# Five raw and three upper-half places for the weight blocks, 42 tokens on gathered rows, and spilled activations at a 1536-byte pitch

## The chip, the core and the metric

The kernel runs on one core of one Trainium2 chip. The metric is the device time of the whole program in microseconds. Three timed runs of the kernel before gave a median of 1625.37 us (1622.57 to 1626.13).

The engines are called as in the profile: PE (TensorE, matrix products), DVE (VectorE), ACT (ScalarE), POOL (GpSimd) and SP (SyncE, which here only issues DMAs). Each runs its own instruction stream in order and waits for the others through counting semaphores.

## The reference, cut to what matters

One decoder layer on 512 tokens of 1024 channels in float32: a mixer (a gated short convolution and an HGRN2 recurrence) with one input and one output projection, a cross-attention into 256 memory tokens, a PEER channel mixer, and a final RMSNorm. The change is in how PEER's first product is shared out; for every token `x`:

```python
q = (tokens @ w_query).reshape(Ntok, 8, 2, 128)
s = einsum('nhpd,hpkd->nhpk', q, sub_keys)          # 16 lists of 128 scores for each token
s_top, i_top = lax.top_k(s, 16)                     # best 16 of each list
cand = s_top[:, :, 0, :, None] + s_top[:, :, 1, None, :]
best, pos = lax.top_k(cand.reshape(..., 256), 16)   # 16 experts of each of 8 heads, of 16384
gate = softmax(best)
a = gelu(sum_d x[n, d] * expert_down[idx[n, k], d]) # one "down" dot product for each chosen expert
out[n] = sum_k gate[n, k] * a[n, k] * expert_up[idx[n, k]]
```

Each token thus needs 128 down dot products (8 heads by 16 experts).

## The kernel before, in words

**Two ways to the same dot products.** The last 128 tokens are "sparse": their chosen rows of `expert_down` and `expert_up` are gathered from HBM by indirect DMAs that POOL issues (one row of 4 KB for each of 128 partitions, 512 KB a gather), and DVE multiplies and sums them. The first 384 tokens are "dense": PE multiplies them by *all* 16384 rows, in 128 blocks of 128 experts, and a matrix of gates that is zero for the experts not chosen picks out what counts. A third group, the EDGE = 32 last of the dense tokens, takes the down products from gathered rows and only the up products from the dense path: for them PE's first product is left out, so that its moving side has DE = 384 - 32 = 352 columns in place of 384.

**The precision.** A float32 product is made of three products of halves: upper by upper, upper by lower, lower by upper (function `three`, L1471 to L1475). So each weight block of 128 by 1024 is loaded raw by SP (`load_block`, `load_down`), then ACT writes its upper half (`high`, L580), POOL its lower half, raw minus upper (`low`, L460), and PE uses both in 24 matmuls (8 chunks by 3, `columns`). Raw, upper and lower places form rings of RING = 4 each, all by block number modulo 4. SP may load block p when block p - 4 has been used; ACT may write the upper half of block p when block p - 4 has been used, but its instruction stands behind one that waits for block p - 3.

**The order of the work.** There is no scheduler: the order is written out by hand, an engine at a time.
- The front (mixer, attention, query projection): 92 weight blocks. 84 are split in halves; 8 are used raw.
- PEER's first product: blocks 0 to 127 of `down`, called first-product blocks here. The first 60 (AHEAD) run while DVE chooses the experts of the three dense tiles (`choose`, with dot products of gathered rows put between its steps). PE transposes the chosen indices of a tile when DVE has them (`turn_indices`, L1790): after block 39, and just before block 59. Blocks 60 to 107 alternate with 48 gate steps (`gate_step`, L1762; DVE builds its one-hot operands in `hots`, L1322 to L1327, at most three steps ahead of PE, and ACT stores the gates to HBM). Blocks 108 to 127 stand alone. ACT applies GELU to each block's result and stores the first 112 to HBM (`hid_dram`), 16 stay on chip.
- PEER's second product: 128 blocks of `up`, 18 matmuls of 512 columns each.

**The dot products of gathered rows** (`dots` on DVE, L1184, `down_row` on POOL, L492). There are ROWS = 128 + 128/4 = 160: 128 for the sparse tokens, and 32 for the edge tokens, whose 32 rows stand four times in the 128 partitions, each copy with a quarter of the 128 experts. A table says how many dots follow each step on DVE, and POOL issues its gathers by the same table: 66 during the choosing (ring A of 7 places), 80 in the gate steps (`DOTS_STEP`), and 14 in blocks 108 to 121, one each (`DOTS_END`). In the last two parts ring B has 4 places: POOL issues 4 rows ahead, and gather k waits until dot k - 4 is done. The instructions of one engine that follow a waiting one wait too: POOL's `low` of the next block stands behind the gathers.

**Storage.** `at(kb, ...)` places a tile at a KB offset in a partition. Two tiles, `kept` (44 KB) and `under_w` (16 KB), hold the raw ring and, beneath the names `w_high` and `w_low`, the halves.

## Time and profile before

| | us |
|---|---|
| median of three timed runs | 1625.37 |
| the profiled execution, its own time | 1627.24 |
| its span, first to last instruction | 1625.5 |
| PE busy | 1601.3 (99%) |
| DVE busy | 1141.6 (70%) |
| POOL busy | 827.5 (51%) |
| ACT busy | 670.8 (41%) |

The span leaves 1.7 us of the execution's own time outside. A matmul's record is longer than the distance to the next one's start, since matmuls overlap in the array; so durations of PE are not added up, and the distance from start to start is what one costs. The granted TensorE clock is 1.00 of 2.4 GHz in every stretch. The transfers move 424.69 MB, 261 GB/s over the span, but unevenly: about 110 GB/s in the front and above 300 GB/s from 520 us on.

### The profile page before, as it was taken

What the parts mean: (1) busy time and instruction counts of PE and PEld (TensorE: products, weight loads), DVE (VectorE), ACT (ScalarE), POOL (GpSimd) and SP (SyncE); (2) the same over time, 40 slices, a digit from 0 to 9 for tenths busy, and PEclk for the clock granted to TensorE, in tenths of its full rate; (3) what the DMA queues carried; (4) which work ended last, traced back from release to release, by engine and by line L of the source; (5) the groups of instructions that cost most, each with busy time, mean ns of one, the idle gap of its engine ahead of it and who ended that gap; (6) DMA issues with size and microseconds to landing.
All of it is one profiled execution on the core that took longest, in us unless ns stands there. A gap on an engine that the chain in (4) does not pass through costs nothing.

```text
span 1625.5 us, 26549 instructions
## 1 busy us (share of the span) xinstructions
PE 1601.3 (99%) x9227; PEld 1423.1 (88%) x9227; DVE 1141.6 (70%) x2214; ACT 670.8 (41%) x998; POOL 827.5 (51%) x523
## 2 busy tenths in 40 slices
PE   8999999999999999999999999999999999999998
PEld 6888888888889999999999999998888888888886
DVE  4155451351519998997999898329888888888887
ACT  5342443441434343534544544334333333333333
POOL 4463386413244988987877777766422222222220
PEclk9999999999999999999999999999999999999999
DMA  4222243313434999997999999949999999999992
GB/s 183 95 99 78 76 146 104 104 40 129 143 104 156 344 324 315 327 327 234 336 403 397 394 408 391 359 149 385 400 358 346 336 348 336 346 337 346 339 334 76
DMA packets 154425, 424.69 MB, mean 261 GB/s; under 512 B 15728, under 2 KB 65904, under 8 KB 154224
## 3 DMA queue, kind: packets, MB, share of 16 engines
q1 hardware_dynamic: 89088, 229.41, 40.5%
q0 software_dynamic: 41472, 151.01, 25.5%
q10 hardware_dynamic: 23792, 43.33, 6.9%
q8 instruction: 42, 0.69, 0.2%
q14 instruction: 31, 0.25, 0.1%
HBM read 379.88 MB, written 43.25 MB: 260 GB/s over the span
## 4 chain that ended last, share of the span: by engine, by line
PE 62%; issue 16%; POOL 10%; DVE 7%; DMA 4%; ACT 1%; POOLq 0%; DVEq 0%; SPq 0%; ACTq 0%
PE psum L1473 19%; PE psum L1474 19%; PE psum L1475 19%; POOL w_low L460 8%; PE psum L1762 4%; DMA kept<-down_in 2%; DVE arena L1184 2%; POOL arena L492 1%; DMA gate_dram<-arena 1%; DMA arena<-down_rows,kept 1%; DVE arena L1204 1%; DVE arena L1195 1%; DVE arena L1196 1%; DVE arena L1260 1%; DVE arena L1191 0%
## 5 line engine op out<-in xcount | busy, mean ns | idle before, releaser
L460 POOL TENSOR_TENSOR w_low<-kept,w_high 128x1024 fp32r<-128x1024 f32 x212 | 519.6, 2454 | 319.0 <-ACT w_high L580 317.1
L1473 PE MATMUL psum<-hT_high,w_high 128*128 128x352 f32 (+2 forms) x1408 | 485.7, 345 | 10.8 <-POOL w_low L460 9.4
L1474 PE MATMUL psum<-hT_low,w_high 128*128 128x352 f32 (+2 forms) x1408 | 477.1, 339 | 0.0
L1475 PE MATMUL psum<-hT_high,w_low 128*128 128x352 f32 (+2 forms) x1408 | 476.5, 338 | 0.0
L580 ACT ACTIVATE w_high<-kept 128x1024 fp32r<-128x1024 f32 x212 | 224.1, 1058 | 223.3 <-DMA kept<-down_in 118.5
L1474 PE MATMUL psum<-up_low,wgt_high 128*128 128x512 f32 x768 | 298.8, 389 | 0.0
L1473 PE MATMUL psum<-up_high,wgt_high 128*128 128x512 f32 x768 | 298.8, 389 | 0.0
L1475 PE MATMUL psum<-up_high,wgt_low 128*128 128x512 f32 x768 | 298.8, 389 | 0.0
L1473 PEld LDWEIGHTS psum<-hT_high,w_high 128*128 128x128 f32 x1408 | 264.5, 188 | 30.4 <-POOL w_low L460 15.1
L1475 PEld LDWEIGHTS psum<-hT_high,w_low 128*128 128x128 f32 x1408 | 265.2, 188 | 12.7
L1474 PEld LDWEIGHTS psum<-hT_low,w_high 128*128 128x128 f32 x1408 | 264.9, 188 | 12.3 <-issue 0.5
L584 ACT ACTIVATE up_high<-arena 128x1024 fp32r<-128x1024 f32 x128 | 135.8, 1061 | 311.7 <-PE psum L1475 305.8
L1184 DVE CUSTOM_DVE_ANT_0 arena<-arena,psum 128x1024 f32<-128x1024 f32 x160 | 190.9, 1213 | 48.9 <-DMA arena<-down_rows,kept 48.7
L1355 DVE TENSOR_TENSOR up_low<-arena,up_high 128x1024 fp32r<-128x1024 f32 x128 | 156.8, 1225 | 76.2 <-ACT up_high L584 76.2
L1475 PEld LDWEIGHTS psum<-up_high,wgt_low 128*128 128x128 f32 x768 | 144.2, 188 | 30.0
L1473 PEld LDWEIGHTS psum<-up_high,wgt_high 128*128 128x128 f32 x768 | 144.2, 188 | 29.8
L1474 PEld LDWEIGHTS psum<-up_low,wgt_high 128*128 128x128 f32 x768 | 144.2, 188 | 29.8
L538 POOL DMA_INDIRECT arena<-up_in,kept x64 | 70.0, 1094 | 180.1 <-DVE kept L1363 166.7
L492 POOL DMA_INDIRECT arena<-down_rows,kept x128 | 121.8, 951 | 67.6 <-DVE kept L1184 37.1
L538 POOL DMA_INDIRECT kept<-up_in,kept x64 | 70.9, 1108 | 166.3 <-DVE kept L1363 157.9
L821 ACT ACTIVATE arena<-psum 128x352 f32<-128x352 f32 x112 | 51.6, 461 | 116.3 <-PE psum L1475 109.2
L1327 DVE TENSOR_TENSOR arena<-arena,psum 128x3072 bf16<-128x3072 bf16 x48 | 83.7, 1744 | 0.0
(252 smaller groups left out, 1960.1 us busy)
## 6 DMA issues: line engine op xcount, KB each, us to landing
kept<-down_in SPq DMA_DIRECT2D x128, 512.0 KB, 6.9
arena<-up_in SPq DMA_DIRECT2D x128, 512.0 KB, 5.6
kept<-front_w SPq DMA_DIRECT2D x92, 512.0 KB, 3.4
gate_dram<-arena ACTq DMA_DIRECT2D x40, 512.0 KB, 10.2
hid_dram<-arena ACTq DMA_DIRECT2D x112, 176.0 KB, 7.0
arena<-hid_dram SPq DMA_DIRECT2D x112, 176.0 KB, 5.0
under_w<-gate_dram SPq DMA_DIRECT2D x24, 640.0 KB, 8.4
arena<-gate_dram SPq DMA_DIRECT2D x8, 640.0 KB, 8.3
```

Of the source, the lines that this page charges most:

```text
L460: nc.gpsimd.tensor_tensor(w_low[:, s, :], ring[:, s, :], w_hi[:, s, :].bitcast(F32), ALU.subtract).then_inc(low_ready, 1)
L492: nc.gpsimd.indirect_dma_start(ring[slot], None, down_rows, bass.IndirectOffsetOnAxis((edge_idx if edge else idx3)[:, j:j + 1].bitcast(U32 ...
L538: nc.gpsimd.indirect_dma_start(rows_c[k % RING_C], None, up_rows, bass.IndirectOffsetOnAxis(idx3[:, k:k + 1].bitcast(U32), 0))\
L580: nc.scalar.activation(w_hi[:, s, :], ring[:, s, :], ACT.Copy).then_inc(high_ready, 1)
L584: nc.scalar.activation(up_hi[:, s % 4, :], uraw[:, up_slot(s), :], ACT.Copy).then_inc(up_high, 1)
L1184: nc.vector.tensor_tensor_reduce(ring[slot], ring[slot], h_row, 1.0, 0.0, ALU.mult, ALU.add, (edge_dot if edge else dot3)[:, j:j + 1]).the ...
L1327: nc.vector.tensor_tensor(hot_g[:, s], hot_i.rearrange("p (n q) i r -> p n q i r", q=1).to_broadcast(each), pieces[:, m:m + PAIRS].rearran ...
L1355: nc.vector.tensor_tensor(up_lo[:, up_slot(s), :], uraw[:, up_slot(s), :], up_hi[:, s % 4, :].bitcast(F32), ALU.subtract).then_inc(up_low, 1)
L1473: nc.tensor.matmul(out, lhs[0], rhs[0], start=first, stop=False)
L1474: nc.tensor.matmul(out, lhs[0], rhs[1], start=False, stop=False)
L1475: return nc.tensor.matmul(out, lhs[1], rhs[0], start=False, stop=last)
L1762: ins = nc.tensor.matmul(psum[:, (2 * h + m) % 3, t % 4 * P:(t % 4 + 1) * P], hot_j[:, h % HOTS, t // 2, :, t % 2], hot_g[:, h % HOTS, t / ...
```

## The change

- **Rings.** The raw ring has five places (RING = 5), the upper halves have three (HIGHS = 3), the lower halves five. A block's place comes from its position p in the order of loads, modulo 5 or modulo 3. SP may load block p when block p - 5 has been used; ACT may write the upper half of block p when block p - 3 has been used. The loops of SP, ACT, POOL and PE over blocks are written out.
- **Edge tokens.** EDGE is 42 in place of 32. 128 partitions hold three copies of 42 tokens (PARTS = 3), so each copy has 43 of the experts (the last 42), and there are 43 edge gathers: ROWS = 171. DE is 342. Edge dots and their operands use 126 partitions (84 in the last one).
- **Where the dots stand.** 70 during the choosing (66, and 4 after the third choice: `DOTS_LULL`), 76 in the gate steps, 25 in blocks 108 to 120, two each and one in the last. GELU of the edge dots comes at gate step 16 (was 12), their use at 23 (was 20).
- **Lower halves on DVE.** For blocks 109, 111, 113, 115 and 117 DVE makes the lower half, not POOL (`dve_low`), with a semaphore of its own.
- **Spilled activations.** `hid_dram` has rows of 384 floats (1536 bytes), of which 342 are written and read; before, rows of 352 (1408 bytes).

```diff
-RING = 4
+RING, HIGHS = 5, 3
-EDGE = 32
+UP_FIRST = 4
+EDGE = 42
 PARTS = P // EDGE
-EDGE_SLOTS = SLOTS // PARTS
+EDGE_SLOTS = -(-SLOTS // PARTS)
-GEL_AT, SPLIT_AT, LAST_TURN = 12, 20, 28
+GEL_AT, SPLIT_AT, LAST_TURN = 16, 23, 28
-DOTS_A = DT * (sum(DOTS_SCORES) + sum(DOTS_CAND) + DOTS_HOT)
-DOTS_STEP = (0, 0) + (2,) * 10 + (1, 2, 2) * 12
-DOTS_END = (1,) * 14
+DOTS_LULL = 4
+DOTS_A = DT * (sum(DOTS_SCORES) + sum(DOTS_CAND) + DOTS_HOT) + DOTS_LULL
+DOTS_STEP = (0, 0, 1) + (2, 2, 1) * 15
+DOTS_END = (2, 2) * 6 + (1,)
...
+        def dve_low(i):
+            return DURING <= i < DURING + 10 and i % 2 == 1
...
+            def load_weights(p):
+                weights = front_w[p if p < FRONT else p + RAW0 - FRONT] if p < USED else down_in[p - USED]
+                if p >= RING:
+                    sp.wait_ge(block_used, p + 1 - RING)
+                sp.dma_start(ring[:, p % RING, :], weights).then_inc(wt[p % RING], 16)
...
-            def high(b, s, landed):
-                act.wait_ge(wt[s], landed)
-                nc.scalar.activation(w_hi[:, s, :], ring[:, s, :], ACT.Copy).then_inc(high_ready, 1)
+            def high(p):
+                act.wait_ge(wt[p % RING], 16 * (p // RING + 1))
+                if p >= HIGHS:
+                    act.wait_ge(block_used, p + 1 - HIGHS)
+                nc.scalar.activation(w_half(p)[0], ring[:, p % RING, :], ACT.Copy).then_inc(high_ready, 1)
...
             for i in range(AHEAD + 2, NK):
-                low(FRONT + i, i % 4)
+                if not dve_low(i):
+                    low(FRONT + i)
                 for _ in range(DOTS_STEP[i - AHEAD] if i < DURING else DOTS_END[i - DURING] if ... else ROWS):
...
+            kd = dots(kd, DOTS_LULL)
...
-            kd = dots(kd, ROWS - kd)
+            for i in range(DURING, DURING + len(DOTS_END)):
+                if dve_low(i):
+                    dve.wait_ge(high_ready, FRONT + i + 1)
+                    high, lower = w_half(USED + i)
+                    nc.vector.tensor_tensor(lower, ring[:, (USED + i) % RING, :], high.bitcast(F32), ALU.subtract)\
+                        .then_inc(end_low_ready, 1)
+                kd = dots(kd, DOTS_END[i - DURING])
...
-    args.append(nc.dram_tensor("hid_dram", (NK, P, DE), F32, kind="Internal").ap())
+    args.append(nc.dram_tensor("hid_dram", (NK, P, DN), F32, kind="Internal").ap())
```

POOL, before, from the `low` of first-product block 108 on (L460 is a lower half, L492 a gather of one expert row for each partition):

```order
L460 TENSOR_TENSOR w_low<-kept,w_high 128x1024 [waits high_ready]
L492 DMA arena<-down_rows,kept 128x1024 [waits dot_done]
L460 TENSOR_TENSOR w_low<-kept,w_high 128x1024 [waits high_ready]
L492 DMA arena<-down_rows,kept 128x1024 [waits dot_done]
L460 TENSOR_TENSOR w_low<-kept,w_high 128x1024 [waits high_ready]
L492 DMA arena<-down_rows,kept 128x1024 [waits dot_done]
```

POOL, in the changed kernel, from the same block on (L470 is the lower half, L499 the gather):

```order
L470 TENSOR_TENSOR w_low<-kept,w_high 128x1024 [waits high_ready]
L499 DMA arena<-down_rows,kept 128x1024 [waits dot_done] x4
L470 TENSOR_TENSOR w_low<-kept,w_high 128x1024 [waits high_ready]
L499 DMA arena<-down_rows,kept 128x1024 [waits dot_done] x4
L470 TENSOR_TENSOR w_low<-kept,w_high 128x1024 [waits high_ready]
L499 DMA arena<-down_rows,kept 128x1024 [waits dot_done] x4
```

The lower half of an even block now stands behind four gathers, each with a wait for a dot product; that of an odd block is no longer on POOL.

DVE, before, from the last one-hot operand of the gate steps on (L1327; L1184 is a dot product with its accumulator read, `ISA` here):

```order
L1327 TENSOR_TENSOR arena<-arena,psum 128x3072 [waits dve_step]
L1184 ISA arena,kept<-arena,psum 128x1024 [waits ld_down_rows_b2]
L1184 ISA kept 128x1
L1184 ISA arena,kept<-arena,psum 128x1024 [waits ld_down_rows_b3]
L1184 ISA kept 128x1
L1184 ISA arena,kept<-arena,psum 128x1024 [waits ld_down_rows_b0]
```

DVE, in the changed kernel, from the same place (L1336 is the operand, L1191 the dot product, L1359 the lower half of block 109):

```order
L1336 TENSOR_TENSOR arena<-arena,psum 128x3072 [waits dve_step]
L1191 ISA arena,kept<-arena,psum 128x1024 [waits ld_down_rows_b3]
L1191 ISA kept 128x1
L1191 ISA arena,kept<-arena,psum 128x1024 [waits ld_down_rows_b0]
L1191 ISA kept 128x1
L1191 ISA arena,kept<-arena,psum 128x1024 [waits ld_down_rows_b1]
L1191 ISA kept 128x1
L1359 TENSOR_TENSOR w_low<-kept,w_high 128x1024 [waits high_ready]
L1191 ISA arena,kept<-arena,psum 128x1024 [waits ld_down_rows_b2]
```

A lower half that PE needs now stands behind dots that wait for gathers, and four dots stand between one such half and the next.

## Rows read from the trace of the kernel before

**Rows 1.** The page: busy time of each engine.
```profile
PE 1601.3 (99%) x9227; PEld 1423.1 (88%) x9227; DVE 1141.6 (70%) x2214; ACT 670.8 (41%) x998; POOL 827.5 (51%) x523
```

**Rows 2.** Windows: length, then PE, PEld, DVE, ACT, POOL busy; clock, DMA share, GB/s.
```profile
0.00:520.00 520.00, 509.75 (x2683) 433.55 (x2684) 213.65 (x435) 217.44 (x351) 229.85 (x111) 1.00 0.33 109
520.00:759.00 239.00, 232.29 (x1424) 227.56 (x1424) 223.82 (x779) 100.89 (x133) 205.26 (x124) 1.00 0.92 316
759.00:1018.00 259.00, 258.60 (x2336) 252.26 (x2336) 239.76 (x318) 126.91 (x199) 199.34 (x135) 1.00 1.00 381
1018.00:1097.00 79.00, 78.50 (x490) 77.70 (x488) 22.21 (x40) 30.64 (x45) 55.00 (x30) 1.00 0.70 250
```

**Rows 3.** Timeline of PE: start, duration in us, line, operation, shape.
```profile
481.73 0.33 PE L1473 MATMUL psum<-hT_high,w_high 128*128 128x384 f32 x1
...
501.49 0.33 PE L1473 MATMUL psum<-hT_high,w_high 128*128 128x384 f32 x1
...
534.75 0.43 PE L1473 MATMUL psum<-hT_high,w_high 128*128 128x352 f32 x1 [0.63 <-POOL w_low L460]
...
538.69 0.32 PE L1473 MATMUL psum<-hT_high,w_high 128*128 128x352 f32 x1
...
557.89 0.32 PE L1473 MATMUL psum<-hT_high,w_high 128*128 128x352 f32 x1
...
735.94 0.32 PE L1473 MATMUL psum<-hT_high,w_high 128*128 128x352 f32 x1
...
1299.83 0.39 PE L1475 MATMUL psum<-up_high,wgt_low 128*128 128x512 f32 x1
...
1322.50 0.39 PE L1473 MATMUL psum<-up_high,wgt_high 128*128 128x512 f32 x1
```

**Rows 4.** Waits, 540 to 759 us: waiter and releaser: total us, times, longest.
```profile
ACT w_high L580 <- DMA kept<-down_in: 85.7, 43, 4.5
...
PEld psum L1473 <- POOL w_low L460: 8.2, 14, 1.3
...
DVE arena L1184 <- DMA arena<-down_rows,kept: 4.6, 2, 3.0
```

**Rows 5.** Timeline of POOL, among the first 60 blocks.
```profile
646.50 0.95 POOL L492 DMA_INDIRECT arena<-down_rows,kept  x1 [0.16 <-issue]
647.75 0.93 POOL L492 DMA_INDIRECT arena<-down_rows,kept  x1 [0.30 <-issue]
...
651.27 0.96 POOL L492 DMA_INDIRECT arena<-down_rows,kept  x1 [0.16 <-issue]
```

**Rows 6.** Timeline: DVE's last piece of the third choice, and PE's turn of it.
```profile
750.55 0.29 DVE L1294 TENSOR_TENSOR arena<-psum,arena 128x128 f32<-128x128 f32 x1
...
759.14 0.71 PE L1790 MATMUL psum<-kept,arena 128*128 128x128 f32 x5
```

**Rows 7.** A window of the gate steps, and its gathers: count, us to landing.
```profile
860.00:920.00 60.00, 60.00 (x530) 58.55 (x529) 57.07 (x76) 29.20 (x47) 45.48 (x33) 1.00 1.03 400
...
arena<-down_rows,kept POOLq DMA_INDIRECT x20, 8.8
```

**Rows 8.** DMA issues, 1018 to 1060 us: count, KB each, us to landing; then every gather's.
```profile
kept<-down_in SPq DMA_DIRECT2D x10, 512.0 KB, 4.5
...
arena<-down_rows,kept POOLq DMA_INDIRECT x9, 7.5
...
DMA to landing us min/median/max: 4.3/8.3/11.4
```

**Rows 9.** Timeline at the end of the gate steps: DVE's dots, PE's block 108.
```profile
1007.90 1.21 DVE L1184 CUSTOM_DVE_ANT_0 arena<-arena,psum 128x1024 f32<-128x1024 f32 x1
...
1018.25 0.41 PE L1473 MATMUL psum<-hT_high,w_high 128*128 128x352 f32 x1
```

**Rows 10.** Timeline: a small DVE operation beside a lower half on POOL.
```profile
729.16 2.43 POOL L460 TENSOR_TENSOR w_low<-kept,w_high 128x1024 fp32r<-128x1024 f32 x1
729.18 2.57 DVE L1243 TENSOR_TENSOR arena<-arena 128x128 bf16<-128x128 uint32 x1
```

More of the change, by code:

```diff
@@ L324, in __call__, with part_slots, part_count, edge_rows @@
                 self.end()
+        def dve_low(i):
+            return DURING <= i < DURING + 10 and i % 2 == 1
+        def part_slots(q):
+            return slice(q * EDGE_SLOTS, min((q + 1) * EDGE_SLOTS, SLOTS))
+        def part_count(q):
+            return min(EDGE_SLOTS, SLOTS - q * EDGE_SLOTS)
+        def edge_rows(j):
+            return EDGE * sum(j < part_count(q) for q in range(PARTS))
         block = ctx.enter_context(nc.Block())
+        def position(b):
+            return b if b < RAW0 else b + RAW
         def up_slot(u):
@@ L378, in _ @@
             for g in range(4):
[L379 to L382 removed]
+                for p in range(USED + NK - 16 + 4 * g, USED + NK - 12 + 4 * g):
+                    load_weights(p)
                 if g == 0:
@@ L467, in kv_low_part @@
                 nc.gpsimd.tensor_tensor(lo, raw, high.bitcast(F32), ALU.subtract).then_inc(kv_low, 1)
-            with pool.Fori(0, 10) as r:
-                for s in range(4):
-                    low(r * 4 + s, s)
+            for b in range(40):
+                low(b)
             for b in range(40, 56):
-                low(b, b % 4)
+                low(b)
                 if b < 46:
@@ L477, in _ @@
                     kv_low_part(b - 54 + 6)
-            with pool.Fori(14, FRONT // 4) as r:
-                for s in range(4):
-                    low(r * 4 + s, s)
+            for b in range(56, FRONT):
+                low(b)
             def down_row(k):
@@ L1475, in three, with columns @@
                 return nc.tensor.matmul(out, lhs[1], rhs[0], start=False, stop=last)
-            def columns(b, s, rhs, n, bank):
-                pe.wait_ge(low_ready, b + 1)
+            def columns(b, rhs, n, bank):
+                pe.wait_ge(low_ready, b + 1 - sum(dve_low(j) for j in range(b + 1 - FRONT)))
                 for k in range(KC):
-                    ins = three(psum[:, bank, 0:n], [w[:, s % 4, k * P:(k + 1) * P] for w in w_half],
+                    ins = three(psum[:, bank, 0:n], [w[:, k * P:(k + 1) * P] for w in w_half(position(b))],
                                 [r[:, k, 0:n] for r in rhs], k == 0, k == KC - 1)
@@ L1541, in keys @@
                     pe.wait_ge(k_out, b - 1)
-                columns(block, block % 4, memT_half, NM, b % 2)
+                columns(block, memT_half, NM, b % 2)
             def values(b0, bank):
@@ L1749, in _, with first_product, gate_step @@
                 ins.then_inc(pk_done, 1)
-            def first_product(i, s):
+            def first_product(i):
                 pe.wait_ge(gelu_out, i + 1)
-                columns(i + FRONT, s, hT_half, DE, 4 + s % 2)
-            def gate_step(n, h):
+                if dve_low(i):
+                    pe.wait_ge(end_low_ready, sum(dve_low(j) for j in range(i + 1)))
+                columns(i + FRONT, hT_half, DE, 4 + i % 2)
+            def gate_step(n):
                 pe.wait_ge(hot_ready, n * 2 + 2)
@@ L1814, in _ @@
                     turn_indices(DT, hk_last, split_last)
-                    first_product(AHEAD + n + 1, (n + 1) % 4)
+                    first_product(AHEAD + n + 1)
                     pe.wait_ge(hkT_out, 2 * DT)
-                gate_step(n, n % 12)
-            with pe.Fori(DURING // 4, NK // 4) as r:
-                for s in range(4):
-                    first_product(r * 4 + s, s)
+                gate_step(n)
+            for i in range(DURING, NK):
+                first_product(i)
             pe.wait_ge(gate_out, 2 * STEPS + 3)
```

203 lines of the change are left out of this document (88 added, 115 removed).

## The prediction

> **What bounds the kernel now.** I read the page's busy times first: PE is busy for 99% of the span, the next engine for 70% [rows 1]. So a microsecond counts only if PE gets shorter or stops waiting. The windows by stage say where PE waits [rows 2]: 10.3 us in the front (520 us long), 6.7 us in the first 60 first-product blocks (520 to 759), 0.4 us in the 48 gate steps (759 to 1018), 0.5 us in the last 20 blocks (1018 to 1097). The same rows show the second pressure: transfers run at 316 and 381 GB/s from 520 us on, and DVE is busy for 224 of 239 and 240 of 259 us. DVE and the DMAs thus have little room just where the change puts work on them. The PE timeline prices a matmul by distances between starts [rows 3]: 114 matmuls of 384 columns in 19.76 us, 173.3 ns each; 120 of 352 in the 19.20 us from 538.69, 160.0 ns; 100 of 512 in 22.67 us, 226.7 ns.
>
> **Term 1, ten columns fewer.** From 352 to 384 columns a column costs 13.3/32 = 0.416 ns, from 384 to 512 53.4/128 = 0.417 ns. It is a straight line, so 342 columns cost 160.0 - 4.2 = 155.8 ns. Each of the 128 blocks has 24 such matmuls, which makes 0.10 us a block: 6.0 us in the first 60, 4.8 us in the gate steps, 2.0 us in the last 20, together 12.8 us if PE stays the bound. From below the line could have a step at 32 columns, which no row between 352 and 384 excludes (gain 0); three points on one line speak against it.
>
> **Term 2, the first 60 blocks.** In the 239 us to the turn of the third choice stand 59 blocks [rows 2, 6], which at 3.84 us (24 x 160.0 ns) are 226.6 us. So 12.4 us go to late blocks. Why: ACT waited 85.7 us, 43 times, for raw blocks to land, and PE's weight loads waited behind POOL's lower half [rows 4]. With a fifth raw place each load is issued a block (3.7 us) earlier, which covers the mean of these waits (2.0 us) and all but the longest (4.5 us). What is late next? First POOL: a second gather costs 1.25 us and a lower half with one gather 3.52 us [rows 5]. Before the change it issued 59 gathers in 52 blocks after its first seven (3.69 us a block), now 63 (3.52 + 0.21 x 1.25 = 3.78 us), just over PE's new 3.74 us. With 0.09 us of jitter I take 3.87 us for blocks 3 to 52, against 4.02 us now (their 50 blocks took from 534.75 to 735.94) [rows 3]: 7.7 us earlier, and 1.1 us in the last six, so PE would reach the turn at about 750.3. Second DVE: its last piece of the third choice ended at 750.84, 8.3 us before PE used it [rows 6], and DVE itself waited only 4.6 us for rows [rows 4], so it can't be much earlier. Both limits coincide: 8.0 us gained (bounds 3, if POOL and the DMAs hold the pace at 4.0 us a block, and 9). The four dots after the choice cost DVE 4.6 us while PE does blocks 59 and 60 (7.5 us) and before its first gate step; they are hidden with about 0.5 us to spare.
>
> **Term 3, the front.** Three upper-half places cost nothing: ACT's instruction for block p stands behind one that waits for block p - 3 already. The fifth raw place can take a little of PE's 10.3 us; most of that is the start. I take 0.5 us (bounds -0.5 and 2).
>
> **Term 4, the gate steps.** DVE's dots there are 76, not 80, and two steps of three with two dots remain; no new DVE limit. The DMAs moved 400 GB/s in the sample window [rows 7], 2.11 MB in a step of 5.29 us. The same bytes in 5.19 us need 407 GB/s. Nothing in 60 us shows more than 400, so I give back 0.5 of the 4.8 us: 4.3 us (bounds 2 and 5). The 1536-byte pitch moves 40 bytes less for each partition, 3% of a stream of 0.18 MB a block: nothing.
>
> **Term 5, the last 20 blocks: the price.** The columns give 2.0 us and a late raw block 0.4 us. But 25 dots now stand where 14 stood, and in blocks 108 to 117 PE needs lower halves that stand behind them: on DVE those of the odd blocks, on POOL those of the even ones, each behind four gathers that wait for dots. Ring B has four places, so four dots take at least one round of a place: the landing, the dot (1.13 us) and 0.2 us to the next issue. A gather took 8.8 us from issue to landing in the gate steps [rows 7] and 7.5 us in this stretch, with half as many gathers [rows 8]. Between them, 8.1: 9.5 us for four, 2.36 us a dot. POOL's lower half (2.4 us) stands in a free place's way once in four, so I take 2.5. Now the race, in the old trace's time: DVE's last gate dot ends at 1009.1 and PE starts block 108 at 1018.25 [rows 9]. The fourth gather goes out at 1009.3, lands at 1018.1, its dot ends at 1019.3. The lower half of block 118 needs dot 20, then an issue and 2.4 us: 1019.3 + 16 x 2.5 + 3.5 = 1062.8. PE without waits would start it at 1018.25 + 10 x 3.75 = 1055.8. So PE loses 7.0 us. With landings of 4.3 us [rows 8] it loses none; with 11.4 us a dot takes 3.35 us and the loss is 20.6 us. In the old trace DVE is busy for only 22 of the 79 us of this stretch, with one dot a block [rows 2]: it is the landings that set the pace, not DVE. The dots end near 1075, before block 124 asks for them. Moving five lower halves off POOL is worth what it saves it there (2.5 us each two blocks); on DVE one costs 1.2 us.
>
> A small DVE operation of 128 elements took 2.57 us beside a lower half on POOL and ended with it [rows 10]; median-sized ones of its kind take 0.3 us. So DVE's lower half could take up to 3.6 us, and four dots with it 8.2 us: still under the 10 us of a gather round, hence no term. GPSIMD Engine Reference, section 1 (Specifications), of the Trainium skill says that GpSimd shares its SBUF interfaces with VectorE and contends with its two-input instructions; by that rule all five halves on DVE may be hit, and the trace's row agrees.
>
> DMA: Bandwidth & Descriptors, section Queues, rings and completion order, of the Trainium skill has each DMA engine take packets in turn from the queues with work. By that rule SP's deeper prefetch would push the gathers back, the raw blocks would land early, and the loss would lie towards the upper bound. The trace fits it: raw blocks land in 4.5 us where gathers take 7.5 [rows 8].
>
> **The sum.** 0.5 + 8.0 + 4.3 + 2.4 = 15.2 us gained, 7.0 lost: 8.2 us. From the profiled execution's 1627.2 us that is 1619.0; the median before (1625.4) lies 1.8 us below that execution, so the median after is 1617.2, say 1617.
>
> **The rivals.**
> - *No stall in the last 20 blocks.* Landings stay under 7 us once the gate stores have ended. For it: they took 7.5 us with up loads beside them, and the least is 4.3. Against: more gathers in flight. It gives the 15.2 us whole, 1610 to 1613.
> - *The first 60 blocks don't shorten.* POOL's 3.78 us and DMAs at 316 GB/s hold the pace; the fifth place only moves the wait. Term 2 is then 3 us, the sum 3.2 us: 1622. For it: the bytes must go through in less time (about 345 GB/s). Against: the gate steps move 400.
> - *Slower.* Ring B, in blocks 108 to 118: with four gathers in flight beside weights and up loads a landing takes 11 us or more, lower halves come late on both engines, and PE loses 20.6 us for 15.2 gained: 1631. It decides from a landing of about 10.6 us, where a dot takes 3.2 us and the loss is 18.
> - *The change doesn't do what it says:* 342 columns cost what 352 do. Then 12.8 us of the gain shrink to what earlier loads give, and the result is within a few us of before, 1622 to 1627. The straight line leaves this little.
>
> **How the numbers follow.** Forecast (a gain of 4 to 11 us, 1614 to 1621) 0.46; no stall 0.24; first 60 not shortened 0.12; slower 0.10; columns for nothing and the rest 0.08. A measurement of this kernel can tell 0.2%, 3.25 us, from no change: below 1622.1 is faster, above 1628.6 slower. Faster: 0.46 + 0.24 + half of 0.12 = 0.76; slower 0.10; same 0.14. The range leaves a tenth on each side: 1609.5 to 1625.
>
> **What would show it.** Starts of 342-column matmuls 156 ns apart. ACT's waits for raw blocks before 759 us down to a third of 85.7, the turn of the third choice about 8 us earlier and within 1 us of DVE's last piece. Steps of 5.19 us. Between blocks 109 and 118 waits of PE for lower halves of DVE and POOL, some 7 us together, and gathers landing in 8 us. Second product unchanged at 226.7 ns. It is wrong if the last 20 blocks show no wait or more than 15 us, if the turn doesn't move, or if PE waits for gates.

## The result, and the profile after

The changed kernel takes 1638.33 us (median of 6 runs, 1636.12 to 1642.73), the kernel before 1626.49 us in runs on the same chip (6 runs, 1622.57 to 1628.01). The ratio is 1.0079, with a 95% interval of 1.0062 to 1.0096. So the change made the kernel 0.8% slower, where 1617 us and "faster" were forecast. All medians and ratios here are of executions in the usual state; one of the twelve of the last kernel below (1748 us, granted clock 0.85) is left out.

The span went from 1625.5 to 1636.1 us. PE's row of the page answers to [rows 1]:

```profile
PE 1598.3 (98%) x9227; PEld 1419.1 (87%) x9227; DVE 1167.6 (71%) x2242; ACT 665.7 (41%) x996; POOL 820.7 (50%) x529
```

PE is busy for 3.0 us less and idle for 13.6 us more. Where, the windows by stage say (they answer to [rows 2]; columns as there):

```profile
520.00:769.00 249.00, 234.87 (x1460) 230.18 (x1460) 235.76 (x793) 101.58 (x134) 210.61 (x129) 0.99 0.92 316
769.00:1020.50 251.50, 251.50 (x2312) 245.42 (x2311) 234.79 (x310) 122.49 (x196) 191.69 (x131) 1.00 1.00 382
1020.50:1103.50 83.00, 76.28 (x461) 74.96 (x459) 39.35 (x60) 28.25 (x41) 55.62 (x35) 0.96 0.75 287
```

The first row ends with block 59 (the turn and its block), the second holds the gate steps, the third the blocks from 108 on. PE idles for 14.1 us in the first and 6.7 us in the third, and there the granted clock is no longer 1.00. From the starts of the blocks on PE I made one table for all kernels of this study: how long the front took, then blocks 0 to 58, blocks 60 to 107 with the gate steps, and blocks 108 to 126. All values are us of the one profiled execution of each; the last column is the median of the timed runs.

| kernel | front | 0 to 58 | gate steps | 108 to 126 | median |
|---|---|---|---|---|---|
| before | 520.1 | 239.6 | 254.7 | 74.5 | 1625.2 |
| after | 521.0 | 244.4 | 251.3 | 83.0 | 1638.3 |
| four raw places | 521.1 | 248.8 | 251.9 | 80.5 | 1638.0 |
| edge 32 | 521.2 | 233.7 | 256.4 | 73.0 | 1619.5 |
| pitch 1368 | 521.0 | 246.1 | 261.1 | 82.4 | 1649.0 |
| store 352 wide | 521.2 | 248.6 | 251.5 | 83.9 | 1641.5 |
| DVE's lower halves back on POOL | 521.0 | 247.6 | 251.7 | 80.2 | 1640.0 |
| last dots spread | 520.8 | 247.4 | 252.0 | 73.1 | 1631.7 |
| gathers spread to block 59 | 520.8 | 235.3 | 256.3 | 80.4 | 1627.3 |
| gathers spread to block 56 | 521.0 | 231.4 | 251.7 | 82.9 | 1624.3 |
| no dots after the last choice | 521.1 | 230.6 | 254.0 | 86.8 | 1630.8 |
| both repairs | 520.8 | 230.6 | 252.1 | 75.9 | 1614.6 |
| both repairs, four raw places | 521.3 | 237.6 | 251.3 | 78.2 | 1624.5 |

Before against after: +0.9, +4.8, -3.4, +8.4, together 10.7 of the 11.8 us by which the medians differ. How finely a cell can be read, the kernels show whose first 60 blocks have the same orders (after, the DVE halves, the spread of the last dots): 244.4 to 247.6. So a cell alone can't tell 3 us.

**The columns.** Two starts on PE's timeline, blocks 122 and 127, answer to [rows 3]:

```profile
1084.54 0.32 PE L1489 MATMUL psum<-hT_high,w_high 128*128 128x342 f32 x1
...
1103.48 0.32 PE L1489 MATMUL psum<-hT_high,w_high 128*128 128x342 f32 x1
```

120 matmuls in 18.94 us are 157.8 ns each, not 155.8.

**The first 60 blocks.** The waits from 520 to 765 us (waiter, what it waited for: total, times, longest) answer to [rows 4]:

```profile
ACT arena L828 <- DMA hid_dram<-arena: 33.6, 14, 6.0
...
POOL arena L499 <- DVE arena L1191: 11.3, 5, 3.7
PE psum L1489 <- POOL w_low L470: 10.9, 9, 3.0
...
PEld psum L1489 <- ACT arena L828: 9.7, 9, 1.8
```

ACT's waits for raw blocks (85.7 us before) have gone: no row of that kind is left. Two small ones have grown: ACT waits for the two places of the spilled activations (1.9 us before), and POOL's gathers wait for dots (0.6 us before). POOL's timeline (the first fence) and DVE's (the second) show the worst place, around block 38; they answer to [rows 5]:

```profile
672.15 2.40 POOL L470 TENSOR_TENSOR w_low<-kept,w_high 128x1024 fp32r<-128x1024 f32 x1
678.26 0.95 POOL L499 DMA_INDIRECT arena<-down_rows,arena  x1 [3.71 <-DVE arena L1191]
679.22 2.38 POOL L470 TENSOR_TENSOR w_low<-kept,w_high 128x1024 fp32r<-128x1024 f32 x1
...
690.03 0.95 POOL L499 DMA_INDIRECT arena<-down_rows,arena  x1 [3.67 <-DVE arena L1191]
```

```profile
672.41 3.18 DVE L1198 MAX8 arena<-arena 128x8 f32<-128x128 f32 x16
675.51 1.22 DVE L1185 TENSOR_TENSOR psum<-arena 126x1024 f32<-126x1024 f32 x1
676.76 1.22 DVE L1191 CUSTOM_DVE_ANT_0 arena<-arena,psum 126x1024 f32<-126x1024 f32 x1
```

DVE is between two of its fixed places for dots: it ends a choice and starts the ranking of the next 16 lists, and from 668.6 to 676.8 us it makes no dot. POOL has filled all seven places, its next gather waits 3.71 us for the dot that ends at 678.0, and the lower half of the next block stands behind that gather. Blocks 38 to 41 take 6.5, 4.8, 7.0 and 5.4 us, block 51 5.3, where 3.79 are due: 10.0 us lost. The turn of the third choice, on DVE and on PE, answers to [rows 6]:

```profile
751.79 0.29 DVE L1301 TENSOR_TENSOR arena<-psum,arena 128x128 f32<-128x128 f32 x1
...
756.56 0.08 DVE L1191 DVE_READ_ACCUMULATOR2_ANT arena<- 126x1 f32 x1
766.76 0.36 DVE L1327 COPY psum<-arena 128x192 f32<-128x192 f32 x1 [10.12 <-ACT arena L849]
```

```profile
764.89 0.71 PE L1808 MATMUL psum<-kept,arena 128*128 128x128 f32 x5
```

DVE had its choice at 752.1 us, PE turned it at 764.9. DVE then idled for 10.12 us: PE was late, not DVE.

**The gate steps** ran at 5.23 us a step. The sample window and its gathers (count, us to landing) answer to [rows 7]:

```profile
860.00:920.00 60.00, 60.00 (x547) 58.56 (x546) 57.64 (x76) 30.29 (x48) 45.34 (x30) 1.00 1.02 394
```

```profile
arena<-down_rows,kept POOLq DMA_INDIRECT x18, 8.4
```

**The last 20 blocks.** DMA issues from 1018 to 1080 us (count, KB each, median us to landing) and DVE's first and last dot of a row of 21 answer to [rows 8, 9]:

```profile
kept<-down_in SPq DMA_DIRECT2D x13, 512.0 KB, 7.4
...
arena<-down_rows,kept POOLq DMA_INDIRECT x19, 8.6
```

```profile
1018.98 1.21 DVE L1191 CUSTOM_DVE_ANT_0 arena<-arena,psum 128x1024 f32<-128x1024 f32 x1
...
1070.21 1.22 DVE L1191 CUSTOM_DVE_ANT_0 arena<-arena,psum 128x1024 f32<-128x1024 f32 x1 [1.01 <-DMA arena<-down_rows,kept]
```

That is 51.23/20 = 2.56 us a dot. Seven distances from the start of a block to the start of the next are too long (from blocks 110, 111, 113, 114, 115, 117 and 118: 4.6, 4.2, 6.4, 5.4, 5.1, 6.2 and 5.4 us), none after them. PE's waits for a lower half, 1020 to 1104 us:

```profile
PE psum L1489 <- POOL w_low L470: 6.1, 4, 2.4
```

All four are for halves made by POOL; no row names one made by DVE. Not all of the loss is idle time. PE's timeline from the end of block 113 to the start of block 114 and on:

```profile
1044.50 0.32 PE L1491 MATMUL psum<-hT_high,w_low 128*128 128x342 f32 x1
1047.23 0.39 PE L1489 MATMUL psum<-hT_high,w_high 128*128 128x342 f32 x1 [2.42 <-POOL w_low L470]
...
1048.80 0.49 PE L1489 MATMUL psum<-hT_high,w_high 128*128 128x342 f32 x1
1049.09 0.49 PE L1490 MATMUL psum<-hT_low,w_high 128*128 128x342 f32 x1
```

```profile
1048.00:1052.00 4.00, 4.00 (x18) 4.00 (x17) 3.36 (x5) 0.51 (x1) 2.05 (x3) 0.57 1.06 402
```

PE waited 2.42 us for a lower half. Soon after it had begun again its starts stood 0.285 us apart, not 0.158, for some 12 matmuls; the granted clock of that window is 0.57, most of it at the lower level of 1.2 GHz. The wait so costs 1.5 us more than itself. The stop of 2.28 us before block 118 was followed by as much, that of 1.19 us before block 116 by none.

### The profile page after: what moved, and what is told of

The parts are those of the page before. It is cut to its first block, busy times and chain, and to the rows that moved or that the text cites. A ratio compares the mean times of both kernels' runs of the same rounds, so it can differ in the third digit from the quotient of the medians.

```text
span 1636.1 us, 25416 instructions
## 1 busy us (share of the span) xinstructions
PE 1598.3 (98%) x9227; PEld 1419.1 (87%) x9227; DVE 1167.6 (71%) x2242; ACT 665.7 (41%) x996; POOL 820.7 (50%) x529
## 2 busy tenths in 40 slices
DMA packets 155940, 429.58 MB, mean 263 GB/s; under 512 B 15834, under 2 KB 65994, under 8 KB 155722
## 4 chain that ended last, share of the span: by engine, by line
PE 73%; DVE 16%; DMA 6%; ACT 2%; POOL 2%; issue 1%; DVEq 0%; ACTq 0%; SPq 0%
PE psum L1489 22%; PE psum L1491 22%; PE psum L1490 22%; DVE arena L1191 5%; DMA arena<-down_rows,kept 4%; PE psum L1780 3%; POOL w_low L470 2%; DVE arena L1211 1%; DVE arena L1202 1%; DVE arena L1203 1%; DVE arena L1198 1%; DVE arena L1207 1%; DMA gate_dram<-arena 1%; PE psum L1725 1%; DVE arena L1231 1%
## 5 line engine op out<-in xcount | busy, mean ns | idle before, releaser
L470 POOL TENSOR_TENSOR w_low<-kept,w_high 128x1024 fp32r<-128x1024 f32 x207 | 506.7, 2452 | 303.5 <-ACT w_high L591 301.8
L1489 PE MATMUL psum<-hT_high,w_high 128*128 128x342 f32 (+2 forms) x1408 | 482.4, 343 | 24.5 <-POOL w_low L470 20.6
L1490 PE MATMUL psum<-hT_low,w_high 128*128 128x342 f32 (+2 forms) x1408 | 476.5, 338 | 0.0
L1491 PE MATMUL psum<-hT_high,w_low 128*128 128x342 f32 (+2 forms) x1408 | 475.6, 338 | 0.0
L1191 DVE CUSTOM_DVE_ANT_0 arena<-arena,psum 128x1024 f32<-128x1024 f32 (+1 forms) x171 | 204.0, 1213 | 28.7 <-DMA arena<-down_rows,kept 28.6
L499 POOL DMA_INDIRECT arena<-down_rows,kept x128 | 124.4, 972 | 75.8 <-DVE kept L1191 45.9
L546 POOL DMA_INDIRECT kept<-up_in,kept x64 | 67.6, 1056 | 166.1 <-DVE kept L1379 156.7
L828 ACT ACTIVATE arena<-psum 128x342 f32<-128x342 f32 x112 | 51.3, 458 | 215.9 <-PE psum L1491 171.5
L1336 DVE TENSOR_TENSOR arena<-arena,psum 128x3072 bf16<-128x3072 bf16 x48 | 83.8, 1746 | 0.0
```

Of the source, the lines that this page charges most:

```text
L470: nc.gpsimd.tensor_tensor(lower, ring[:, p % RING, :], high.bitcast(F32), ALU.subtract).then_inc(low_ready, 1)
L499: nc.gpsimd.indirect_dma_start(ring[slot], None, down_rows, bass.IndirectOffsetOnAxis((edge_idx if edge else idx3)[:, j:j + 1].bitcast(U32 ...
L546: nc.gpsimd.indirect_dma_start(rows_c[k % RING_C], None, up_rows, bass.IndirectOffsetOnAxis(idx3[:, k:k + 1].bitcast(U32), 0))\
L828: nc.scalar.activation(hid[i % 2], psum[:, 4 + i % 2, 0:DE], ACT.Gelu).then_inc(gelu_out, 1)
L1191: nc.vector.tensor_tensor_reduce(ring[slot][0:rows], ring[slot][0:rows], h_row[0:rows], 1.0, 0.0, ALU.mult, ALU.add, (edge_dot if edge els ...
L1336: nc.vector.tensor_tensor(hot_g[:, s], hot_i.rearrange("p (n q) i r -> p n q i r", q=1).to_broadcast(each), pieces[:, m:m + PAIRS].rearran ...
```

## The experiments

Each ratio is against the kernel before in the same batch of runs, on the same chip. The batches ran on three chips, where the median of the kernel before was 1624.1 to 1625.2 us, and the changed kernel was timed only in the batch of the section above (1626.5 us for the kernel before). A difference to the changed kernel in us is one of medians of two batches; by the ratios it comes out up to 1.3 us otherwise. The theory after the first look: 42 edge tokens lose time in two places, since the orders around them fill up (gathers in the first 60 blocks, the last 25 dots), while the rings gain. The rivals: the rings gain nothing, the columns cost as before, the spill stores are the cause.

**What a column costs.** Block i has the width of its place in a row of eight:

```diff
-                columns(i + FRONT, hT_half, DE, 4 + i % 2)
+                columns(i + FRONT, hT_half, (342, 352, 344, 336, 340, 338, 348, 346)[i % 8], 4 + i % 2)
```

> The changed kernel with the moving side of the first product 342, 352, 344, 336, 340, 338, 348, 346 columns wide by block number modulo 8 (columns that a block leaves out are not computed, so the output is not the reference's). Linear theory: starts 0.4167 ns a column apart, so 342 costs 155.8 ns, 344 156.7, 336 153.3, 348 158.3, 352 160.0. Step theory: the moving side is served in groups of columns, so some widths share a price; 342 measured 157.9 ns in the changed kernel, which is what 347 columns would cost. Groups of 4: 342 and 344 alike at 156.7, no match. Groups of 16: 338 to 352 all at 160.0, 336 at 153.3. Rival: a width that is no multiple of 4 (or 8) pays about 2 ns by itself: 342, 338, 346 two ns above the line and 344, 336, 340, 348, 352 on it.

Mean distance between starts inside a block, in ns, of one execution:

| 336 | 338 | 340 | 342 | 344 | 346 | 348 | 352 |
|---|---|---|---|---|---|---|---|
| 153.6 | 156.1 | 154.9 | 157.5 | 157.2 | 159.4 | 158.3 | 160.5 |

The multiples of four lie within 0.5 ns of the line from 336 to 352, 0.43 ns a column. The others (338, 342, 346) lie 1.3 to 1.6 ns above that line; 342 columns cost no less than 344. The rival was right: the straight line holds between multiples of four only.

**Four raw places.**

```diff
-RING, HIGHS = 5, 3
+RING, HIGHS = 4, 3
```

> The changed kernel with four raw places and three upper-half ones; all else as changed. Theory A (DVE's choosing sets the pace of the first 60 blocks, because POOL's gathers wait for DVE's dots and the lower halves stand behind them): the fifth place is worth little; ACT waits for raw blocks again, about 80 us, but block 59 starts within 2 us of the changed kernel's 765.4, and the time is within 3 us of 1638. Theory B (the fifth place is what pays in the first 60 blocks): block 59 starts 5 to 8 us later and the time is about 1645. Theory C (the fifth place hurts, as its loads crowd out spill stores and gathers): block 59 starts 4 us or more earlier and the time is about 1633.

1637.95 us (4 runs), ratio 1.0075 (1.0058 to 1.0092): as the changed kernel, as theory A had it. But ACT's waits for raw blocks were back (74.0 us in 38 waits) and block 59 came 4.4 us later, between what theories A and B had, and the last stage gave 2.5 us back. Both are within what such cells scatter. In this kernel the fifth place could not be told from nothing; that was not the last word (the last run below).

**Edge 32 with the new rings.** The changed kernel's rings, loops and pitch, with the edge and the orders of the kernel before:

```diff
-EDGE = 42
+EDGE = 32
-DOTS_LULL = 4
+DOTS_LULL = 0
-DOTS_STEP = (0, 0, 1) + (2, 2, 1) * 15
-DOTS_END = (2, 2) * 6 + (1,)
+DOTS_STEP = (0, 0) + (2,) * 10 + (1, 2, 2) * 12
+DOTS_END = (1,) * 14
```

> The rings of the changed kernel (five raw places, three upper halves, loops written out, 1536-byte pitch) with the edge of the kernel before: 32 tokens, 352 columns, 160 dots in the old places, no lower half on DVE. If the 42 tokens are what costs (dots, gathers), this is as fast as the kernel before or faster: 1620 to 1626, with block 59 at 752 to 757 (4 to 8 us earlier than before) and no waits of PE in the last 20 blocks. If the rings or the written-out loops cost, it is slower than before: over 1630, with PE's waits in the first 60 blocks above 12 us as in the changed kernel.

1619.46 us (6 runs), ratio 0.9966 (0.9954 to 0.9979): faster than before by 5.5 us. Blocks 0 to 58 take 5.9 us less than before, POOL waits for hardly a dot. So rings and pitch are a gain, and the ten edge tokens more, with their orders, cost 19 us.

**Spilled tiles at a pitch of 1368 bytes**, as wide as their content:

```diff
-    args.append(nc.dram_tensor("hid_dram", (NK, P, DN), F32, kind="Internal").ap())
+    args.append(nc.dram_tensor("hid_dram", (NK, P, DE), F32, kind="Internal").ap())
```

> The changed kernel with spilled rows of 342 floats one after another (1368-byte pitch). If the pitch matters, the spill stores (median 5.7 us and at most 13.0 us to landing in the first 60 blocks of the changed kernel) land later, ACT waits longer than 33 us for them, and the time rises by 2 us or more over 1638; if not, all stages are as in the changed kernel and the ratio to it is 1 within 0.2%.

1648.99 us (4 runs), ratio 1.0151 (1.0124 to 1.0179): 10.7 us more than with 1536. ACT's waits for these stores go from 33.6 to 59.6 us before 765 us, the median of a store there from 5.7 to 6.9 us, with the same count of packets and the same bytes (155940 packets, 429.58 MB in both). Most of the loss (9.8 us) falls in the gate steps: five of them take 6.6 to 8.6 us where the changed kernel has 5.2.

**Store 352 columns, multiply 342**, at 1536 bytes:

```diff
+                cols = 352 if i < 100 else DE
-                act.dma_start(hid_dram[i, :, 0:DE], hid[i % 2])
+                act.dma_start(hid_dram[i, :, 0:cols], hid[i % 2][:, 0:cols])
```

> The changed kernel, but each of the first 100 spilled activation tiles is stored 352 columns wide (1408 bytes for each partition) in place of 342 (1368 bytes). The ten columns more are never read, the pitch stays 1536 bytes and all matmuls stay at 342 columns. Theory A: 1408 bytes are 22 whole pieces of 64 bytes, 1368 are 21 and a rest, and a write that ends in a rest is slow; it is why ACT waited 33.6 us for its spill stores before 765 us in the changed kernel and 14.5 us in the kernel with 352 columns and the same rings. Then the waits fall to about 15 us, block 59 starts 3 to 5 us earlier than 765.35, and the time is 1633 to 1635. Rival B: the stores wait because the transfers are more crowded (42 edge tokens take gathers and dots with them); forty bytes more for each partition make it no better: waits of 30 us or more, and 1637 to 1640.

1641.5 us (4 runs), ratio 1.0095 (1.0076 to 1.0114), not faster than the changed kernel. ACT's waits fell only to 25.3 us and nothing came of it. Theory A fell: the end of the rows is not what this kernel waits for. In the run before, the pitch alone changed. Whether it hurts by where rows begin, by pieces that two rows share, or by where the tile lies in memory wasn't tried.

**Gathers of the first 60 blocks spread later.**

```diff
-while k < DOTS_A and i > FIRST_GATHER and (k - RING_A) * (AHEAD - 8 - FIRST_GATHER) < (i - FIRST_GATHER - 1) * (DOTS_A - RING_A):
+while k < DOTS_A and i > FIRST_GATHER and (k - RING_A) * (AHEAD - 1 - FIRST_GATHER) < (i - FIRST_GATHER - 1) * (DOTS_A - RING_A):
```

> The changed kernel, but GpSimd spreads its gathers of the first 60 blocks up to the last block, not up to eight blocks before the end. Theory A: GpSimd's gathers come too early for VectorE's dots (it waited 11.3 us in five waits, up to 3.7, with lower halves queued behind, and blocks 38, 40 and 51 took 5.3 to 7.0 us). Later gathers wait less: 5 us at most, blocks 38 to 41 lose 5 us less, block 59 starts 2 to 4 us earlier, and the time is 1634 to 1636. Rival B: the spread only moves the waits; now VectorE waits for rows near the turn, the last choice ends later, and PE gets there no sooner: 1637.5 to 1641.

1627.33 us (10 runs), ratio 1.0010 (0.9998 to 1.0023): 11 us gained by one number, more than theory A asked. POOL's waits for dots fell from 12.8 to 0.6 us (the row of 11.3 us above and a smaller one of the same kind), blocks 38 to 41 no longer stand out, block 59 starts at 756.03. One new stop of 4.7 us stands before block 10: there ACT waited 7.0 us for a spill store, so such a wait can reach PE. But now the four rows for the dots after the last choice come too late. The waits of this kernel from 755 to 770 us:

```profile
DVE arena L1191 <- DMA arena<-down_rows,arena: 6.5, 3, 4.0
...
PEld psum L1780 <- DVE arena L1336: 3.7, 1, 3.7
```

DVE waits for rows, PE for DVE's first gate operands, and block 60 takes 9.9 us, 4.7 more than in the changed kernel.

**DVE's lower halves back on POOL.**

```diff
-return DURING <= i < DURING + 10 and i % 2 == 1
+return False
```

> The changed kernel, but none of the five lower halves of blocks 109 to 117 is moved to VectorE: GpSimd makes them all, as in the kernel before. Theory A: they were worth something, since each costs GpSimd 2.4 us in a stretch where a dot takes 2.56 us on average and its lower halves stand behind gathers: PE waits 3 to 6 us more in the last 20 blocks (11.0 us now), 1641 to 1644. Rival B: what sets the pace there is the round of a ring place (landing, dot, issue); the lower half stands behind the same dots on either engine, so nothing changes: 1637 to 1640. A third way: VectorE's dots come sooner without the halves in between, and it gets faster, under 1636.

1640.0 us (4 runs), ratio 1.0094 (1.0077 to 1.0111), which overlaps the changed kernel's: rival B. The last stage was even shorter (80.2 against 83.0 us). The moved halves neither help nor harm by an amount that this shows.

**The last dots spread.**

```diff
-DOTS_END = (2, 2) * 6 + (1,)
-return DURING <= i < DURING + 10 and i % 2 == 1
+DOTS_END = (2, 1) * 8 + (1,)
+return DURING <= i < DURING + 16 and i % 2 == 1
```

> The changed kernel, but the 25 dots of the last 20 blocks are spread as 2, 1, 2, 1, ... over 17 blocks (now 2, 2, ... over 13), and VectorE makes the lower half of every odd block of the first 16 (now of the first 10). Theory A: a dot takes 2.56 us there whatever the plan. The lower half of block 118 then needs dot 15, not 20, and is due 12.8 us earlier, so PE's loss (11.0 us of waits now) falls to 2 or 3 us; dots end near 1083 us, before block 125 needs them. The time is 1629 to 1631. Rival B: PE's waits there come from late raw blocks and the slow stores beside the up loads, not from the plan; then the waits stay above 8 us and the time is 1636 to 1640.

1631.65 us (5 runs), ratio 1.0046 (1.0030 to 1.0062): 6.7 us gained by the medians, 5.4 by the ratios, nearly all that theory A gave. The window of the last blocks:

```profile
1024.00:1097.00 73.00, 72.41 (x460) 71.85 (x458) 40.67 (x63) 28.03 (x41) 50.50 (x32) 1.00 0.85 327
```

PE idles for 0.6 us there (6.7 in the changed kernel) and the granted clock is 1.00. The same 25 dots, the same ring of four: the plan asked for them too early.

**Gathers spread to block 56.** As above with `AHEAD - 4`: the old pace, and the rows for the last four dots still in time.

> The changed kernel, but GpSimd spreads the 63 gathers of the first 60 blocks up to four blocks before the turn: one in 0.87 blocks, the pace that the kernel before had (59 in 51 blocks), in place of 0.81; the four rows more come in the last four blocks. Theory A: a pace ahead of VectorE's dots was the whole fault of the first 60 blocks. Then GpSimd waits for dots 2 us or less (11.3 in the changed kernel), block 59 starts near 756 us (as with the latest spread, 756.03), and since the four extra rows have landed by 752 us, the first gate step doesn't wait as it did there (9.9 us for 5.2). Block 108 starts near 1012 (1020.5 in the changed kernel), the time is 1623 to 1629. Rival B: what helped in the latest spread was fewer transfers at the start; then GpSimd's waits come back in part and the time is 1630 or more.

1624.3 us (10 runs), ratio 1.0000 (0.9987 to 1.0012). Theory A in all its points, POOL's waits for dots (1.1 us) included: block 59 at 752.4, a first gate step of 5.2 us, block 108 at 1008.0. The waits of this kernel from 520 to 765 us:

```profile
ACT arena L828 <- DMA hid_dram<-arena: 47.0, 22, 4.0
...
PEld psum L1489 <- ACT arena L828: 5.4, 6, 1.4
PE psum L1489 <- POOL w_low L470: 3.4, 4, 1.2
```

ACT now waits *longer* for its stores than in the changed kernel (47.0 us for 33.6), and PE reaches block 59 13 us earlier. So these waits were slack for the most part, the tallest row of waits for a transfer and yet not the cause. In the stretch of the third ranking PE idled for 5.7 us in the changed kernel and does not here (windows of the changed kernel, then of this one):

```profile
675.00:695.00 20.00, 14.29 (x86) 13.55 (x85) 19.97 (x97) 6.72 (x10) 12.37 (x9) 0.97 0.85 282
```

```profile
672.00:691.00 19.00, 19.00 (x124) 18.98 (x123) 18.96 (x80) 8.25 (x12) 17.80 (x12) 1.00 0.97 328
```

**No dots after the last choice.**

```diff
-DOTS_LULL = 4
-DOTS_STEP = (0, 0, 1) + (2, 2, 1) * 15
+DOTS_LULL = 0
+DOTS_STEP = (1, 2, 2) + (2, 2, 1) * 15
```

> The changed kernel, but the four dots that follow the last choice stand in the first gate steps (1, 2, 2, ... for 0, 0, 1, ...), and so GpSimd issues 59, not 63, gathers in the same 51 blocks, the kernel before's pace, by its own rule. Theory A (pace): GpSimd's waits for dots in the first 60 blocks go (2 us or less), block 59 starts near 756 us, 9 us earlier; VectorE has 4.8 us more in the first gate steps, which PE feels there as 3 to 5 us: 1630 to 1634. Rival B: it is the wider gathers (42 tokens a part, 126 rows) or the narrower, denser block that cause the waits, and with 59 gathers they stay above 8 us: 1637 or more.

1630.83 us (7 runs), ratio 1.0045 (1.0029 to 1.0062). The first 60 blocks are mended by the other way to the same pace (block 59 at 751.75), the first gate steps pay 2.7 us, and the last stage is 3.9 us longer than the changed kernel's. Rival B is out: the gathers are as wide and the blocks as narrow as in the changed kernel, and the waits have gone (1.1 us left).

The last stage of this kernel shows what was missed before. POOL's, DVE's and PE's timelines at block 111:

```profile
1021.79 2.38 POOL L470 TENSOR_TENSOR w_low<-kept,w_high 128x1024 fp32r<-128x1024 f32 x1
```

```profile
1022.52 2.74 DVE L1359 TENSOR_TENSOR w_low<-kept,w_high 128x1024 fp32r<-128x1024 f32 x1
```

```profile
1025.37 0.39 PE L1489 MATMUL psum<-hT_high,w_high 128*128 128x342 f32 x1 [2.51 <-issue]
```

DVE's half began beside POOL's, took 2.74 us and not 1.22, and PE went on 0.11 us after its end. Four of the five halves on DVE were stretched in this way (3.08, 2.74, 1.58 and 3.05 us, 5.6 us in all over 1.22 each), and each of PE's stops before blocks 109, 111, 113 and 115 ended 0.1 us after one of them. That is enough for the 3.9 us. It is read from one trace; no run keeps the two apart.

**Both repairs**, `AHEAD - 4` and the spread last dots.

> The changed kernel with both repairs: gathers spread up to four blocks before the turn, and the 25 last dots as 2, 1, 2, 1, ... with VectorE's lower halves in every odd block of the first 16. Theory A: the two losses are apart and add up. The end spread alone gave 6.7 us against the changed kernel, the pace 11 us or more: 1618 to 1621, under the kernel before (1625) and about the kernel with 32 edge tokens (1619.5). Rival B: the gate steps' stream of dots is what both feed, and the gains overlap: 1623 to 1627.

1614.64 us (6 runs, 1613.26 to 1617.71), ratio 0.9940 (0.9925 to 0.9954). The gains add up; the end spread alone is worth 9.7 us here, against the kernel without it in the same batch (1624.3). This version beats the kernel before by 9.5 us and the changed one by 23.7 (22.6 by the ratios). Against the kernel with 32 edge tokens (1619.46 us, ratio 0.9966) the ten edge tokens more now gain 4 to 5 us net.

**Both repairs with four raw places.**

> The kernel with both repairs (gathers spread up to four blocks before the turn, last dots 2, 1, 2, 1, ...), but with four raw places in place of five. It prices the fifth place where the gathers no longer hide it. Theory A: the raw waits (74 us in 38 waits with the unrepaired order) come back and PE feels a part: block 59 starts 4 to 6 us later than 751.45 (the difference was 4.4 us in the unrepaired order), the last 20 blocks lose nothing: 1618 to 1621 for 1614.6. Rival B: in the whole the fifth place is worth nothing (with the unrepaired order the two times were the same, 1638.3 and 1638.0), since what it gives at block 59 the gate steps and the end take back: 1613 to 1616.5.

The median is 1624.5 us (11 runs), ratio 0.9993 (0.9982 to 1.0003). ACT's row from 520 to 765 us:

```profile
ACT w_high L591 <- DMA kept<-down_in: 89.7, 45, 4.5
```

So the fifth place is worth about 9 us once nothing hides it (9.9 by the medians, 8.6 by the ratios; the two intervals, 0.9925 to 0.9954 and 0.9982 to 1.0003, stand well apart), 7.0 of them before block 59 by the table. Theory A had the place and too small a number; rival B is out.

## Why the prediction was wrong, by its own steps

The sign was wrong. Forecast was a gain of 8.2 us, measured a loss of 11.8. The step that failed is term 2, in its clause on POOL (12.8 us off), and terms 1 and 5 were mis-sized.

**Term 2, forecast -8.0 us, measured +4.8.** The first half of the step was right: the raw waits went, and what they cost is now shown (7.0 us before block 59, by four against five places with both repairs). What failed is "First POOL: ... 3.52 + 0.21 x 1.25 = 3.78 us". I priced what four gathers more cost POOL in its own time, and never asked whom they wait for. Ring A has seven places, which DVE's dots free. DVE's dots stand at fixed places between its ranking steps, unchanged; all four new dots stand after the last choice. POOL spreads its gathers evenly, so the four extra ones made it issue *all* of them earlier: one in 0.83 blocks for one in 0.88 (63 and 59 gathers over the same 52 blocks). It ran into DVE's stretches without dots with a full ring, waited 11.3 us in five waits, and the lower halves stood behind. What would have shown it was at hand: DVE's timeline with its stretch without dots, and this row of the waits of the kernel before, 520 to 765 us, by which the two already met at the old pace:

```profile
POOL arena L492 <- DVE arena L1184: 0.6, 3, 0.3
```

At about the old pace the same kernel reaches block 59 at 752.4 (gathers spread to block 56) and 751.8 us (no dots after the last choice); the forecast had PE's turn at 750.3. The range of the term (3 to 9 us of gain) had no end below nothing.

**Term 1, forecast 12.8 us, measured 6.8.** 24 x (160.0 - 157.8) ns is 0.053 us a block, for 128 blocks. The line through 352, 384 and 512 columns was right for multiples of four. I weighed a step at 32 columns and not a finer one.

**Term 3, forecast -0.5, measured +0.9.** Every kernel with the new code has a front of 520.8 to 521.3 us, with four raw places too, so the fifth place gave nothing there. The cause stays open.

**Term 4, forecast -4.3, measured -3.4.** The step is 5.23 us and not 5.19, which is term 1's error. My give-back for DMA rates was not needed as such: the sample window moved 394 GB/s. No new DVE limit appeared, and one did when four dots came late.

**Term 5, forecast -2.4 + 7.0 = +4.6, measured +8.4.** The mechanism was right for POOL's halves, down to the dot: 2.56 us for 2.5, landing 8.6 us for 8.1, no stall after block 118. Block 118 started 9.4 us late (1067.82 against 1020.52 + 10 x 3.79), for 7.0 forecast; with what its own block loses the stage's excess over 19 x 3.79 is 10.9 us. Of that 6.7 us are idle. Most of the rest is slower matmuls, and this was missing from the sum: each of the two longest stops was followed by matmuls at the lower clock level. What the prediction had wrong in the mechanism is DVE's part: its five halves never kept PE waiting in this kernel. The columns gave 1 us here, not 2.0.

**DVE beside POOL.** The prediction allowed DVE's lower half up to 3.6 us. Four of the five took 1.22 us; the fifth ran beside one of POOL's, on both timelines:

```profile
1055.21 2.38 POOL L470 TENSOR_TENSOR w_low<-kept,w_high 128x1024 fp32r<-128x1024 f32 x1
```

```profile
1056.35 2.33 DVE L1359 TENSOR_TENSOR w_low<-kept,w_high 128x1024 fp32r<-128x1024 f32 x1
```

It took 2.33 us and ended 1.09 us after POOL's. The Trainium skill says that GpSimd and VectorE contend for shared SBUF interfaces (GPSIMD Engine Reference, section 1); the trace agrees where the two meet, and in this kernel they met once. With the halves put back on POOL nothing got better, so for this kernel the allowance was rightly no term. With other orders it was one: four halves took up to 3.08 us in the kernel with no dots after the last choice, and PE waited for them.

**The queues.** The prediction drew from the Trainium skill (DMA: Bandwidth & Descriptors, section Queues, rings and completion order) that raw blocks would land early and gathers late. In the stretch of [rows 8], 1018 to 1060 us, raw blocks took 7.7 us from issue to landing, for 4.5 before, and gathers 8.7 for 7.5: both got slower, at 400 GB/s for 355. So raw blocks did not land early. No run here tells how the engines shared their turns.

**The rivals.** "First 60 not shortened" (0.12) had the right place and too mild a form. "Slower" (0.10) was placed in the last 20 blocks, where 8.4 us did come, but not by landings of 10.6 us; that the time fell on its side of the forecast is no merit of it. "342 columns cost what 352 do" was half true. That several losses could come together was not priced, and 0.76 for "faster" was far too sure.

The 1536-byte pitch was put at nothing. Against 1368 bytes, the natural pitch of 342 columns, it is worth 10.7 us (11.7 by the ratios); against the 1408 bytes of the kernel before it was not tried alone.

## What to carry to other kernels

When a change adds work to an in-order engine that fills a ring, compare its pace with the pace of the engine that *frees* the ring, stretch by stretch; an even spread over a longer list moves every item earlier, also past those the new items have nothing to do with. A row of waits that is small and not zero says that the two already meet somewhere, and a tall row may be slack: here 47 us of waiting for stores went with the faster kernel. Price a stop of PE at more than its length if the trace shows the clock fall after one. And when work moves to another engine, look at whether its pieces now run beside each other.

## What the runs showed of the hardware

- A float32 matmul whose columns are no multiple of four (338, 342, 346) costs 1.3 to 1.6 ns more than the line from 336 to 352 columns: 342 columns 157.5 ns, 344 columns 157.2 ns.
- Rows of 1368 bytes written side by side cost this kernel 10.7 us more than the same rows at a pitch of 1536 bytes, with equal packets and bytes (a store in the first 60 blocks took 6.9 us for 5.7). Writing 1408 in place of 1368 bytes at that pitch brought nothing.
- After a stop of 2.42 us PE ran on at full pace for about 1.3 us and then for 3.4 us with starts 0.285 us apart, at a granted clock of 0.57 over that window.
- A subtraction of 128x1024 on DVE with both inputs in `kept` and `w_high` took 1.22 us alone. In all 13 traced cases where it began 0.13 to 2.00 us before the end of a like one on POOL, it ended 1.08 or 1.09 us after POOL's: it stood still until POOL's was done, up to 3.08 us in all. POOL's own took its usual 2.4 us. The one time that DVE's began first, POOL's took 3.00 us. A dot product on DVE beside POOL's subtraction (at 1055.21 us in the changed kernel) took its usual 1.22 us.
